# Sparse heads in natural order, the index's rounds moved back, and seven squares added on VectorE

## The reference

```python
def hybrid_layer(x, ...):
    h = rms_norm(x, attn_norm)
    aq, ak, av, iq, ik, iw, bq, bk, bv, gates = split_cols(h @ w_in)
    ...
    ya = sparse_attention(aq, ak, av, iq, ik, iw, k_sel)    # 8 heads, k_sel = 128 of 512 keys
    ...
    yb = diff_attention(bq, bk, bv, lam)                    # 4 heads, two score maps each
    ...
    merged = g_a * (ya @ w_up_a) + g_b * (yb @ w_up_b)
    x = x + merged @ w_out
    h = rms_norm(x, ffn_norm)
    gate, up = jnp.split(h @ w_ffn_in, 2, axis=-1)
    return x + (jax.nn.silu(gate) * up) @ w_ffn_out
```

## Time and profile before

| | |
|---|---|
| median of 3 runs | 2478.55 us (2477.89 to 2478.76) |
| profiled execution | 2477.99 us, span 2476.5 us |
| PE busy | 2300.4 us, 93% |
| VectorE busy | 1240.2 us, 50% |
| ScalarE busy | 840.0 us, 34% |
| GpSimd busy | 362.5 us, 15% |

### The profile page before, as it was taken

One profiled execution on the slowest core, in us unless ns is written; L12 is line 12 of the kernel. 1 busy time (PEld: TensorE's weight loads), 2 busy tenths in 40 slices (PEclk: granted clock), 3 DMA queues, 4 the chain that ended last, 5 costly groups with the idle time before them and its releaser, 6 DMA issues.

```text
span 2476.5 us, 28622 instructions
## 1 busy us (share of the span) xinstructions
PE 2300.4 (93%) x11077; PEld 1727.6 (70%) x11077; DVE 1240.2 (50%) x2286; ACT 840.0 (34%) x1478; POOL 362.5 (15%) x273
## 2 busy tenths in 40 slices
PE   7899988789889989999999999999789999999999
PEld 5785676454334766678778888787567777888887
DVE  5543456431113787673544434448776445443442
ACT  4334433321102435444333212334454333332221
POOL 0111123000000543332000000035332310000000
PEclk9999999889999999999999999999999999999999
DMA  8116300269997121221222323222122212323222
GB/s 291 52 52 223 101 27 10 94 241 334 368 383 257 60 77 60 60 69 52 85 86 94 102 94 98 81 81 73 56 60 68 68 52 94 94 94 96 91 94 77
DMA packets 198569, 281.61 MB, mean 114 GB/s; under 512 B 13308, under 2 KB 125732, under 8 KB 198436
## 3 DMA queue, kind: packets, MB, share of 16 engines
q1 hardware_dynamic: 197872, 278.60, 33.7%
q10 hardware_dynamic: 564, 1.18, 0.1%
HBM read 277.65 MB, written 2.10 MB: 113 GB/s over the span
## 4 chain that ended last, share of the span: by engine, by line
PE 72%; DVE 15%; DMA 5%; ACT 5%; issue 2%; SPq 1%; POOL 0%; DVEq 0%; ACTq 0%
PE PS L620 19%; PE PS L622 18%; PE PS L621 18%; PE PS L2225 3%; PE PS L1377 2%; PE PS L2265 2%; PE PS L1359 1%; PE PS L2156 1%; DVE AL L823 1%; PE PS L680 1%; DMA RX<-in_w_up_dram 1%; DVE AL L815 1%; DMA RAW<-in_w_up_dram 1%; PE PS L2281 1%; DVE AL L802 1%
## 5 line engine op out<-in xcount | busy, mean ns | idle before, releaser
L620 PE MATMUL PS<-OPH,WHI 128*128 128x512 f32 x1224 | 504.4, 412 | 12.4 <-DVE OPL L1413 7.7
L622 PE MATMUL PS<-OPH,WLO 128*128 128x512 f32 x1224 | 485.6, 397 | 0.0
L621 PE MATMUL PS<-OPL,WHI 128*128 128x512 f32 x1224 | 483.2, 395 | 0.0
L575 ACT ACTIVATE WHI<-RAW 128x1024 fp32r<-128x1024 f32 (+2 forms) x286 | 294.2, 1032 | 464.2 <-PE PS L622 455.1
L608 POOL TENSOR_TENSOR WLO<-RAW,WHI 128x1024 fp32r<-128x1024 f32 (+1 forms) x107 | 253.2, 2371 | 1331.5 <-ACT WHI L575 1328.1
L592 DVE TENSOR_TENSOR WLO<-RAW,WHI 128x1024 fp32r<-128x1024 f32 x179 | 214.7, 1201 | 396.3 <-ACT WHI L575 396.2
L620 PEld LDWEIGHTS PS<-OPH,WHI 128*128 128x128 f32 x1224 | 232.8, 190 | 84.1 <-issue 33.9
L622 PEld LDWEIGHTS PS<-OPH,WLO 128*128 128x128 f32 x1224 | 232.5, 190 | 52.4
L621 PEld LDWEIGHTS PS<-OPL,WHI 128*128 128x128 f32 x1224 | 233.2, 190 | 46.8 <-issue 2.4
L620 PE MATMUL PS<-WHI,OPH 128*128 128x512 f32 (+2 forms) x576 | 237.0, 412 | 10.2 <-ACT AL L757 3.6
L621 PE MATMUL PS<-WLO,OPH 128*128 128x512 f32 (+2 forms) x576 | 222.9, 387 | 0.0
(11 more groups left out here) (400 smaller groups left out, 3328.8 us busy)
## 6 DMA issues: line engine op xcount, KB each, us to landing
RAW<-in_w_in_dram SPq DMA_DIRECT2D x102, 512.0 KB, 3.5
RAW<-in_w_ffn_in_dram SPq DMA_DIRECT2D x88, 512.0 KB, 3.5
RX<-in_w_gate_dram SPq DMA_DIRECT2D x42, 512.0 KB, 7.3
RX<-in_w_down_dram SPq DMA_DIRECT2D x42, 512.0 KB, 11.4
RAW<-in_w_ffn_out_dram SPq DMA_DIRECT2D x40, 512.0 KB, 3.4
RAW<-in_w_mod_dram SPq DMA_DIRECT2D x36, 512.0 KB, 4.6
RX<-in_w_up_dram SPq DMA_DIRECT2D x32, 512.0 KB, 10.5
RAW<-in_w_up_dram SPq DMA_DIRECT2D x25, 512.0 KB, 9.2
```

Of the source, the lines that this page charges most:

```text
L575: hi.up(A.e.activation(q.fhi, q.flat, ACT.Copy), ("w", q.i))
L620: T.e.matmul(o, a[0], b[0], start=first, stop=False)
L621: T.e.matmul(o, a[0], b[1], start=False, stop=False)
L622: return T.e.matmul(o, a[1], b[0], start=False, stop=last)
```

## The change

The sums of squares at "out", "out2" and "ffo" of layer 0: ScalarE writes the square of column 0 into slot 0 and all others into slot 1; VectorE adds slot 1 to slot 0 for columns 1 to 6; PE multiplies slot 0 by the ones once, after column 7's matmuls, and then the square of column 7. The expert stage keeps its own. The bank of the sum is taken then, where it was taken at the first column.

The index: `index_at` takes no step in the first two groups of `bq`, three in the rest of `bq` and in `bk`, and one (before three) in each group of `bv`. `best_at` is rewritten: of steps 0 to 15 rounds stand at 1, 2, 3, 9, 14 and 15, none at 16 and 17, two and one by turns at 18 to 31, two at 32 to 37. The sparse query blocks run 0, 1, 2, 3 in place of 1, 2, 3, 0. In the second layer all stands as in the first.

```diff
@@ -360,6 +360,7 @@
     copied = Either(copy_v, copy_a)
     set_v, set_a = signal("set_v"), signal("set_a")
     sq, root, rstd = signal("sq"), signal("root"), signal("rstd")
+    squares = signal("squares")
     scaled, nhi, nlo = signal("scaled"), signal("nhi"), signal("nlo")
     split_a, split_v = signal("split_a"), signal("split_v")
     row_a, row_v, row_p = signal("row_a"), signal("row_v"), signal("row_p")
@@ -2050,11 +2051,33 @@
             nlo.up(V.e.scalar_tensor_tensor(OPL[:, m, :], XT[:, m, :], gain, OPH[:, m, :].bitcast(F32),
                                               ALU.mult, ALU.subtract), (nm, m))
 
-        def dve_add_cols(key, columns, gate, nm=None):
+
+
+        def act_square_added(key, m, SQ):
+            if m >= 2:
+                A.wait_ge(*squares[key, m - 1])
+            sq.up(A.e.activation(SQ[:, min(m, 1), :], XT[:, m, :], ACT.Square), (key, m))
+
+        def dve_square_added(key, m, SQ):
+            if m > 1:
+                V.wait_ge(*squares[key, m - 1])
+            V.wait_ge(*sq[key, m])
+            squares.up(V.e.tensor_tensor(SQ[:, 0, :], SQ[:, 0, :], SQ[:, 1, :], ALU.add), (key, m))
+
+        def pe_sum_added(key, SQ):
+
+            PB[key] = B.one()
+            B.clear(PB[key])
+            T.wait_ge(*squares[key, 6])
+            T.e.matmul(ps(PB[key]), C("ones"), SQ[:, 0, :], start=True, stop=False)
+
+        def dve_add_cols(key, columns, gate, nm=None, SQ=None):
             for c, pieces in enumerate(columns):
                 for i in pieces:
                     dve_lo(i + 3)
                 for m in (2 * c, 2 * c + 1):
+                    if SQ is not None and m >= 2:
+                        dve_square_added(key, m - 1, SQ)
                     dve_add(key, m, gate)
                     if nm and m:
                         dve_gained(nm, m - 1)
@@ -2070,15 +2093,15 @@
                         A.wait_ge(*added[key, m])
                         if nm:
                             act_gained(nm, m)
-                        act_square(key, m, XT, SQ, 512)
+                        act_square_added(key, m, SQ)
             if stat:
                 act_root(key, 512, RST)
 
         def pe_add_cols(key, columns, rhs, operand, SQ, stat):
 
             def after(m):
-                if stat and m:
-                    pe_sum(key, m - 1, SQ, 512)
+                if stat and m == 7:
+                    pe_sum_added(key, SQ)
 
             pe_cols(key, columns, rhs, 512, operand, lambda m: [(added, (key, m))], after)
 
@@ -2099,7 +2122,7 @@
             act_add_cols("out", OUT1, SQO, True)
 
         def dve_out():
-            dve_add_cols("out", OUT1, lambda m: mod[:, 2, m, 0:1])
+            dve_add_cols("out", OUT1, lambda m: mod[:, 2, m, 0:1], None, SQO)
             dve_rstd("out", 512, RST)
 
 
@@ -2592,8 +2615,7 @@
 
                     if m in (1, 2):
                         pe_rope_turns(first + rows_turned(n, m))
-                    if n != "bq" or m >= 2:
-                        some(index_, 3)
+                    some(index_, index_at(n, m))
 
         def rows_turned(n, m):
             return {"bq": 4, "bk": 8, "bv": 12}[n] - (2 if m == 1 else 0)
@@ -2711,8 +2731,7 @@
         SPARSE = ("aq", "ak", "av")
         GATES0, TURN0, UPB0 = 48, 112, 120
 
-
-        SPARSE_ROWS = (1, 2, 3, 0)
+        SPARSE_ROWS = (0, 1, 2, 3)
 
         def sparse_tokens(blk):
             i = SPARSE_ROWS[blk - 4]
@@ -2919,7 +2938,10 @@
 
         parts_at = lambda s: 3 if s < 32 else 2
 
-        best_at = lambda s: (1 if s < 8 else 1 - s % 2 if s < 16 else 1 if s < 30 else 2 if s < 32 else 0)
+
+        best_at = lambda s: 1 if s in (1, 2, 3, 9, 14, 15) else 2 - s % 2 if 18 <= s < 32 else 2 if 32 <= s < 38 else 0
+
+        index_at = lambda n, m: 0 if n == "bq" and m < 2 else 1 if n == "bv" else 3
         OUT2 = 7
 
         def units2(l):
@@ -3188,7 +3210,7 @@
                         dve_merged_low(l, m - 1)
             dve_merged_low(l, 7)
 
-            dve_add_cols(("out2", l), J["out2", l], lambda m: 0.5, ("fn", l))
+            dve_add_cols(("out2", l), J["out2", l], lambda m: 0.5, ("fn", l), SQ4)
 
         def dve_merged_low(l, m):
             V.wait_ge(*mix_a["mt", l, m])
@@ -3280,7 +3302,7 @@
                         V.wait_ge(*glu_a["hi", l, m])
                         glu_v.up(V.e.tensor_tensor(AF[1][:, m % 20, :], SLU[:, j, :], AF[0][:, m % 20, :].bitcast(F32),
                                                    ALU.subtract), ("lo", l, m))
-                dve_add_cols(("ffo", l, f), J["ffo", l, f], None, ("an", 1) if f == 1 and l == 0 else None)
+                dve_add_cols(("ffo", l, f), J["ffo", l, f], None, *((("an", 1), SQ5) if f == 1 and l == 0 else ()))
 
 
         OR = ORM[:, :].rearrange("p (t f) -> p t f", t=4)
```

## The result

Five runs of the changed kernel gave a median of 2456.25 us (2448.72 to 2464.66) against 2478.47 (2476.47 to 2478.76); the ratio is 0.9909, 95% interval 0.9884 to 0.9935. It is faster by 22 us, where 37 were forecast, and the median lies 2.3 above the range. The same kernel run again, beside three experiments, gave 2448.33 (2445.23 to 2453.58) against 2479.19: 0.9878 (0.9864 to 0.9893), 31 us; that median lies inside the forecast range of 2432 to 2454, though still 6 us short of the 37 in the sum.

A forecast was written before the change was run, and what follows sets the result against it. TensorE (PE), busy 2300.4 of 2476.5 us, was taken as the bound, VectorE at attention's start. Terms −21.8 − 19.2 − 3.4 + 2.6 + 2.1 + 2.6 − 1.6 + 1.5 gave −37.2, to 2441.3; range 2432 to 2454.

The forecast's parts named there:

- The squares: At "out", both "out2" and "ffo" of layer 0: fewer ones-matmuls on PE, less new waits for adds, −21.8 us.
- Start of attention: Fewer rounds before unit 1: gains 8.6 (layer 0) and 10.6 (layer 1), −19.2; 1.5 given back for possible half clock.
- Dense units: Units 0 to 15: stalls before unit 9 and behind unit 12's round shrink, −1.7 a layer, −3.4 us.
- The round at unit 15: Last round of i = 1 and its mask ahead of L2877 lengthen PE's wait of 1.1, +2.6 for two layers.
- PE's own work only changes places: Units 16 to 47: reordered widths leave PE's work the same; the 128-wide units' stall of 0.75 goes, −1.6.
- The added rounds: More VectorE rounds from unit 18 on: +2.1 around units 20 to 23, +2.6 from 1.3 of wait at unit 38.
- Rival B: Expert stage: the loads of the experts take back what "out" gives, +5.2, 2446.5; 8%.
- D: Clock is half at both starts of attention: +7 less the 1.5 counted, 2447; 10%.
- G: Two-input VectorE operations on PE's path held 2.0 each by GpSimd splits, five a layer: +20, 2461; 8%.
- E: VectorE leads more of the dense units' stalls, up to 5 more a layer: −10, 2431; 8%.
- C: VectorE becomes the bound in every pair of units 18 to 37, 3.7 a pair: about 2510; 4%.
- three signs named for being wrong: PE's waits in units 18 to 39 up over 6 a layer; adds taking 2 us; stalls over 5 at bv's end.

The follow-up runs named there:

- E3: Kernel before with sparse order 0 1 2 3 and the changed kernel's places of rounds, squares as before; 2479.72 us against 2479.19, ratio 1.0001.
- E2: Kernel before with only the sparse order changed, 0 1 2 3 for 1 2 3 0; 2489.88 us against 2479.19, ratio 1.0044.
- again: Second profiled execution of the unaltered changed kernel, run beside three experiments; median 2448.33 us against 2479.19, ratio 0.9878.
- E9: Changed kernel with the rounds behind unit 17 thinned out, none at unit 20; 2444.79 us against 2478.09, ratio 0.9868.
- E7: Kernel before with sparse order 0 2 3 1, rounds and squares as before; 2479.76 us against 2478.35, ratio 1.0010.
- E1: Changed kernel with the sparse order and places of rounds of the kernel before, so squares alone; 2452.91 us against 2479.19, ratio 0.9898.

## Why the prediction was wrong

**The squares: right.** Forecast 21.8 (its terms 5.2, 2 × 5.0 and 6.7 add up to 21.9); the stretches of the changed kernel show 4.7 + 5.1 + 7.3 + 5.2 = 22.3. The wait at "ffo" was 1.58 (1.5 to 1.6 forecast), at "out2" 0.40 (0.2).

**Start of attention: right.** Forecast 8.6 and 10.6 (1758.01 − 1747.5 is 10.5); measured 8.9 and 10.3. The clock stayed at 2.4 GHz, so the 1.5 given back was not needed. That the banks of layer 1 would stand as in layer 0 agrees with the two waits at L861 above, and with E3, where they don't.

**Dense units: right in size, in part by luck.** Forecast −1.7 a layer, measured −2.2 and −2.5. But of the 1.1 that was to go behind the round of unit 12, only 0.3 went (the wait of 1.3 to 1.4 became 1.0 to 1.1). The rest came in units 7 to 9, 0.9 and 1.5 less in the two layers, and in unit 11, 0.8 and 0.7; what gave way there stays open.

**The round at unit 15: right in place and size, short in what followed.** The wait grew from 1.1 to 2.6, by 1.5 for 1.27; 0.2 of it stands in E2 too, where the rounds are the old ones. In layer 0 of the profiled execution the clock fell behind it (0.59), which in "again" it did not: 26.8 against 25.5.

**"PE's own work only changes places": the step that failed.** The forecast went from equal work to equal time, and took 1.6 off for the stall of the 128-wide units (twice 0.75 is 1.5). The work is indeed the same; the time isn't. These are windows of layer 0 from unit 16 to the end of attention, for before, E9 and E2 (the columns of the earlier trace rows, PE's busy time second):

```profile
1026.21:1194.47 168.26, 160.98 (x861) 128.33 (x861) 90.94 (x204) 67.06 (x133) 43.27 (x18) 1.00 0.20 60
...
1012.97:1183.36 170.39, 161.00 (x862) 128.27 (x861) 110.90 (x250) 66.39 (x133) 43.20 (x18) 1.00 0.20 59
...
1024.92:1197.60 172.68, 163.90 (x861) 131.14 (x861) 91.05 (x204) 67.04 (x133) 43.18 (x18) 0.98 0.20 59
```

At the full clock PE is busy 161.0 in either order. E2, which changes the order alone, adds 1.5 of idle time and 2.9 of busy time at a clock of 0.98. It shows three places at which the balance breaks; each layer costs 4.1 to 4.4 where −0.8 had been written. First, where VectorE held PE (units 20 and 21, VectorE busy 10.42 of 11.87 in the earlier trace rows), units 20 to 23 gave 0.8 to 1.0 of the 1.7 that their narrower matmuls save (PE busy 21.2 there before, 19.5 in E7). Second, PE's wait at unit 42 was forecast to go (−0.8), since it was 0.75 at 128 columns; it became 2.5 at 512. Steps 40 to 43 have no pieces of dense matmuls to hide it, only turns (L3045), and the maximum of unit 41 stands in VectorE's queue behind a scaling and two splits of OPL, and the splits wait for ScalarE. The rows are of the changed kernel, ScalarE and then VectorE:

```profile
1140.22 0.72 ACT L3146 ACTIVATE AL<-AL,AC 128x512 f32<-128x512 f32 x1 [3.41 <-DVE AC L1384]
...
1141.56 1.06 ACT L1410 ACTIVATE OPH<-PS 128x512 fp32r<-128x512 f32 x2
```

```profile
1142.16 1.29 DVE L1414 TENSOR_TENSOR OPL<-PS,OPH 128x512 fp32r<-128x512 f32 x2 [0.86 <-ACT OPH L1410]
1143.37 0.68 DVE L2918 TENSOR_TENSOR AL<-PS,RST 128x512 f32<-128x512 f32 x1
1143.97 0.68 DVE L1384 CUSTOM_DVE_ANT_0 AL<-PS,AL 128x512 f32<-128x512 f32 x1
```

Third, PE ran at half clock behind that wait. In the eight profiles with the new order, two layers each, units 42 and 43 took 5.2 three times, 6.5 to 6.6 ten times and 7.8 to 8.0 three times, always behind a wait of 2.5: the half clock cost nothing, 1.3 to 1.5, or 2.6 to 2.9. E7 supports the role of the width (0.56 in place of 1.73 for units 40 and 41); that the queue of VectorE is what makes it 2.5 was read from these rows, and a kernel with the splits elsewhere wasn't tried.

**The added rounds: right in size.** Their terms were 1.3, 1.05 and 1.3 a layer, 3.65. Between E2 and the changed kernel, which have the same order, units 16 to 47 differ by 4.4 in layer 0, of which 1.3 is half clock, and by 3.6 in layer 1; units 20 to 23 by 0.7 and 0.9, units 32 to 38 by 1.1. What the forecast did not see is that the rounds which had stood there already cost PE their length too: PE waited 1.8 at unit 22 in E2, and E9, with none at unit 20, has no such wait.

**The sum.** Units 16 to 47 cost 8.8 and 7.6 in the profiled execution, 16.5 where 5.7 had been written. Of these 10.8, 10.1 are the order (4.4 + 4.1 in E2, where −1.6 had been written). The profiled execution missed the forecast by 10.7 (26.5 of 37.2). That the two figures agree so closely is in part luck: the squares, the dense units and the 1.5 not needed for the clock came out 3.3 better than forecast, and the expert stage and the stretch up to "out", where the changed kernel does the same work as before, took 2.9 longer.

The other 4.3 us by which the median of 2456.25 missed have no trace, as only one of the five runs was profiled, and their cause stays open. What is on record is that the slower runs were granted less clock: 0.976 on average at 2448.72 and 2451.56, 0.973 and 0.972 at 2456.25 and 2456.34, 0.967 at 2464.66. The profiles here also differ by up to 6.1 in the stretch up to "out" and by 4.4 in the expert stage, in kernels that do the same there. The 95% interval of five runs is 12 us wide.

Rival B (swallowed gain) did not show in the means of E1; D (half clock at the starts) and G (adds held by GpSimd) did not come: no add took over 0.69. Of E (more of the dense stalls, up to 5 a layer) 0.5 and 0.8 came. C did not come either; VectorE held PE at units 16, 22, 38 and 42, not in every pair. None of the three signs named for being wrong came: PE's waits in units 18 to 39 grew by 1.3 in layer 0, since the wait that grew most, at unit 42, lies outside.

## What to carry to other kernels

When units of different cost change places, ask of each place what hides their chain there, not only whether the work adds up: a narrow unit gains less where another engine sets the pace (0.8 to 1.0 of 1.7), and a wide one costs more where the cover has run out (a wait of 2.5 for 0.75). Rounds of background work cost nothing or their full length by where they stand: two rounds less at unit 20 gave their full 2.5 us a layer and one more at unit 19 took its full 1.25, while units 24 to 31 took 40.7 us with ten rounds (E2), twelve (changed) and sixteen (E9). Where whole runs scatter by 10 us and more, compare stretch by stretch between fixed instructions before you explain a median.

## What was not expected of the hardware

TensorE ran at half clock behind one and the same wait in some executions and not in others. Behind 2.5 us of idleness units 42 and 43 took 5.2, 6.6 or 7.9 us; behind 2.6 us units 16 to 19 took 25.5, 26.8 or 28.3. In E3 both long values stand in layer 0 and both short ones in layer 1: 5.5 us between two layers of one execution with the same instructions. The Trainium skill, "TensorE: Matmul & The Clock Gate", Part 1, gives half rate as the state of an idle engine, and calls the number of matmuls that run slow when a kernel starts variable from run to run; the traces here show such a spread behind a wait in the middle of a kernel.
